# State space groups: one weighted decay matrix per head in place of two, and x left unweighted

## What is computed

```python
xdt = x * dt[..., None]
decay = segsum_exp(a_dt)
cb = jnp.einsum('bclgn,bcsgn->bcgls', c, b)
y_diag = jnp.einsum('bcgls,bcgrls,bcsgrp->bclgrp', cb, decay, xdt)
decay_states = jnp.exp(a_cs[..., -1:] - a_cs)
states = jnp.einsum('bclgn,bcgrl,bclgrp->bcgrpn', b, decay_states, xdt)
...
y_fwd = ssd_scan(xs, dt[:, :, 0], a[0], bs, cs)
y_bwd = fl(ssd_scan(fl(xs), fl(dt[:, :, 1]), a[1], fl(bs), fl(cs)))
y = y_fwd + y_bwd + xs * d_skip.astype(jnp.float32).reshape(G, R, 1)
```

## Time and profile before

| | |
|---|---|
| median of 3 runs | 1942.93 us (1938.41 to 1943.11) |
| profiled execution, its own time | 1937.86 us |
| its span (first to last instruction) | 1936.1 us |
| granted TensorE clock, mean | 0.982 |
| PE busy | 1826.7 us (94%) |
| PEld busy | 1510.2 us (78%) |
| DVE busy | 901.8 us (47%) |
| ACT busy | 856.2 us (44%) |
| POOL busy | 854.7 us (44%) |

### The profile page before, as it was taken

One profiled execution on the slowest core, in us unless ns is written; L12 is line 12 of the kernel. 1 busy time (PEld: TensorE's weight loads), 2 busy tenths in 40 slices (PEclk: granted clock), 3 DMA queues, 4 the chain that ended last, 5 costly groups with the idle time before them and its releaser, 6 DMA issues.

```text
span 1936.1 us, 27496 instructions
## 1 busy us (share of the span) xinstructions
PE 1826.7 (94%) x9012; PEld 1510.2 (78%) x9012; DVE 901.8 (47%) x1308; ACT 856.2 (44%) x1796; POOL 854.7 (44%) x598
## 2 busy tenths in 40 slices
PE   5899999999899999999999999989989999999988
PEld 4688788878687878778888888867878888877766
DVE  4588887878514565223432033060171111545654
ACT  4455555555234656323443244243523332556542
POOL 4355555555553131444444444454484444441312
PEclk9999999999999999999999999999999999999989
DMA  4731211212133131333223333324232223221111
GB/s 157 122 96 56 64 59 60 61 59 59 39 108 116 34 103 38 106 107 98 76 92 95 97 97 98 101 76 150 76 94 81 87 87 100 75 90 45 54 33 55
DMA packets 46218, 159.78 MB, mean 83 GB/s; under 512 B 4763, under 2 KB 7195, under 8 KB 45884
## 3 DMA queue, kind: packets, MB, share of 16 engines
q1 hardware_dynamic: 38592, 140.53, 23.6%
q10 hardware_dynamic: 7548, 18.20, 3.8%
HBM read 152.42 MB, written 6.29 MB: 82 GB/s over the span
## 4 chain that ended last, share of the span: by engine, by line
PE 59%; issue 19%; DVE 9%; POOL 6%; ACT 2%; DVEq 0%; DMA 0%; POOLq 0%; ACTq 0%
PE main L294 48%; POOL w_lo L257 5%; DVE u_acc L1830 2%; PE aux L779 2%; PE main L322 2%; PE main L1664 1%; PE aux L611 1%; PE aux L1741 1%; PE aux L766 1%; PE aux L364 1%; PE aux L635 1%; DVE vv L2056 1%; DVE x_res L555 1%; PE aux L753 1%; POOL spare_lo L269 1%
## 5 line engine op out<-in xcount | busy, mean ns | idle before, releaser
L257 POOL TENSOR_TENSOR w_lo<-raw,w_hi 128x512 fp32r<-128x512 f32 x504 | 714.0, 1423 | 968.0 <-ACT w_hi L253 954.3
L253 ACT ACTIVATE w_hi<-raw 128x512 fp32r<-128x512 f32 x486 | 303.8, 630 | 707.8 <-PE main L294 693.9
L294 PE MATMUL main<-w_hi,a_hi 128*128 128x512 f32 x752 | 316.1, 420 | 2.3 <-ACT vv L1434 1.4
L294 PE MATMUL main<-w_hi,a_lo 128*128 128x512 f32 x752 | 298.1, 396 | 0.0
L294 PE MATMUL main<-w_lo,a_hi 128*128 128x512 f32 x752 | 297.5, 396 | 0.0
L294 PE MATMUL main<-a_hi,w_hi 128*128 128x512 f32 x576 | 231.2, 401 | 3.2 <-ACT u_raw L1193 3.2
L294 PE MATMUL main<-a_hi,w_lo 128*128 128x512 f32 x576 | 226.4, 393 | 0.0
L294 PE MATMUL main<-a_lo,w_hi 128*128 128x512 f32 x576 | 225.9, 392 | 0.0
L294 PEld LDWEIGHTS main<-w_hi,a_lo 128*128 128x128 f32 x752 | 143.5, 191 | 31.7
L294 PEld LDWEIGHTS main<-w_hi,a_hi 128*128 128x128 f32 x752 | 144.2, 192 | 29.9 <-issue 2.1
L294 PEld LDWEIGHTS main<-w_lo,a_hi 128*128 128x128 f32 x752 | 144.3, 192 | 23.7
(11 more groups left out here) (293 smaller groups left out, 3123.4 us busy)
## 6 DMA issues: line engine op xcount, KB each, us to landing
raw<-w_stream_in SPq DMA_DIRECT2D x264, 512.0 KB, 3.5
x_res<-x_in ACTq DMA_DIRECT2D x8, 512.0 KB, 5.0
rel_rows<-rel_row ACTq DMA_DIRECT2D x1, 4096.0 KB, 45.6
bias<-rel_rows ACTq DMA_DIRECT2D x2, 1536.0 KB, 8.4
out<-x_res SPq DMA_DIRECT2D x4, 512.0 KB, 2.6
bgate<-b_gate_in ACTq DMA_DIRECT2D x4, 256.0 KB, 5.2
ln_g<-ln_g_in ACTq DMA_DIRECT2D x1, 1024.0 KB, 5.4
ln_b<-ln_b_in ACTq DMA_DIRECT2D x1, 1024.0 KB, 7.5
```

Of the source, the lines that this page charges most:

```text
L253: eng.activation(w_hi[:, k, :], raw[:, k, :], ACT.Copy).then_inc(hi_done, 1)
L257: eng.tensor_tensor(w_lo[:, k, :], raw[:, k, :], w_hi[:, k, :].bitcast(F32), ALU.subtract).then_inc(lo_done, 1)
L294: mm = eng.matmul(mb[m][:, :], lhs, rhs, start=(first and k == 0 and n == 0), stop=(last and k == KT - 1 and n == 2))
```

## The change

The two directions' dt go into the matrix instead of into x: M = (dt_f * cb_m[0] + dt_b * cb_m[1]) * decay, one matrix per head, and PE multiplies it with `x_tok` itself.

- ACT: a new `scale_cb` per head, four Copy activations of 128 x 128 from SBUF to SBUF with dt of the forward direction as scale. Those of heads 0 and 1 stand on either side of `decay_exp` 3, those of heads 2 and 3 behind `w_hi` of slots 1 and 2.
- DVE: `xdt` is gone. `weigh` is four scalar_tensor_tensor of 128 x 128, a wait for the last of them, and one tensor_tensor of 128 x 512.
- PE: `pe_y` has one matmul per chunk instead of two.
- POOL: `xw` is made from `x_tok`, with `e_st` multiplied by dt once, early, by one DVE operation of 128 x 256. It waits for `x_tok` instead of `xdt`.

```diff
         def pe_y(eng, g, r, half):
             if r == 0:
                 eng.wait_ge(arg_done, g * 4 + 4)
+                eng.wait_ge(aux_free[0], g * 5 + 2)
+                eng.wait_ge(aux_free[1], g * 5 + 2)
             eng.wait_ge(t_done, g * 4 + r + 1)
             for c in range(NT):
-                for dr in range(2):
-                    x = eng.matmul(ab[c // 2][:, (c % 2) * GW + r * HP:(c % 2) * GW + r * HP + HP],
-                                   dmat[r][:, dr, c * P:c * P + P], xdt[:, dr, c, r * HP:r * HP + HP],
-                                   start=(dr == 0), stop=(dr == 1))
+                x = eng.matmul(ab[c // 2][:, (c % 2) * GW + r * HP:(c % 2) * GW + r * HP + HP],
+                               dmat[r][:, 0, c * P:c * P + P], x_tok[:, c, r * HP:r * HP + HP], start=True, stop=True)
...
+                pool.wait_ge(aux_free[0], g * 5 + 2)
+                pool.wait_ge(aux_free[1], g * 5 + 2)
+                pool.wait_ge(dt_dve, 7)
                 for dr in range(2):
-                    pool.wait_ge(xdt_done, g * 2 + dr + 1)
-                    pool.tensor_tensor(xw[:, dr].rearrange("p c (r q) -> p c r q", r=R), xdt[:, dr].rearrange("p c (r q) -> p c r q", r=R),
+                    pool.tensor_tensor(xw[:, dr].rearrange("p c (r q) -> p c r q", r=R), x_tok[:, :, :].rearrange("p c (r q) -> p c r q", r=R),
                                        per_head(e_st, 0, NT, dr, g), ALU.mult).then_inc(xw_done, 1)
...
+            def scale_cb(g, r):
+
+                if r == 0:
+                    act.wait_ge(aux_free[1], g * 5 + 1)
+                for c in range(NT):
+                    cs = slice(c * P, c * P + P)
+                    x = act.activation(dmat[r][:, 0, cs], cb_m[:, 0, cs], ACT.Copy, scale=dt_sb[:, c, bass.ds(g * R + r, 1)])
+                x.then_inc(cb_scaled, 1)
+
...
                 slots(0, 1)
+                scale_cb(g, 0)
                 decay_exp(g, 3)
+                scale_cb(g, 1)
                 if not last:
                     pick_rows(g + 1, 1 - half)
-                slots(1, 4 - half)
+                slots(1, 2)
+                scale_cb(g, 2)
+                slots(2, 3)
+                scale_cb(g, 3)
+                slots(3, 4 - half)
...
                 def weigh(r):
+                    dve.wait_ge(cb_scaled, g * 4 + r + 1)
+                    for c in range(NT):
+                        cs = slice(c * P, c * P + P)
+                        x = dve.scalar_tensor_tensor(dmat[r][:, 0, cs], cb_m[:, 1, cs], dt_sb[:, c, bass.ds(g * R + (NH + r), 1)],
+                                                     dmat[r][:, 0, cs], ALU.mult, ALU.add)
+                    ch(x)
                     dve.wait_ge(decay_done, g * 4 + r + 1)
-                    dve.tensor_tensor(dmat[r][:, :, :], cb_m[:, :, :], dmat[r][:, 1:2, :].broadcast_to((P, 2, TOK)), ALU.mult).then_inc(t_done, 1)
+                    dve.tensor_tensor(dmat[r][:, 0, :], dmat[r][:, 0, :], dmat[r][:, 1, :], ALU.mult).then_inc(t_done, 1)
...
-                dve.wait_ge(aux_free[0], g * 5 + 2)
-                dve.wait_ge(aux_free[1], g * 5 + 2)
-                for dr in range(2):
-                    dve.tensor_tensor(xdt[:, dr].rearrange("p c (r q) -> p c r q", r=R), x_tok[:, :, :].rearrange("p c (r q) -> p c r q", r=R),
-                                      per_head(dt_sb, 0, NT, dr, g), ALU.mult).then_inc(xdt_done, 1)
                 arg_min(g, 3)
```

More of the change, by code:

```diff
@@ L154, in two_blocks @@
         dmat = [at(f"dmat{h}", B0 + (20 + 4 * h) * KB, [P, 2, TOK]) for h in range(R)]
-        xdt = at("xdt", B0 + 36 * KB, [P, 2, NT, GW])
         xw = at("xw", B0 + 44 * KB, [P, 2, NT, GW])
@@ L571, in two_blocks @@
         aux_free = [sem("aux2_free"), sem("aux3_free")]
-        xdt_done, xw_done, skip_done = sem("xdt_done"), sem("xw_done"), sem("skip_done")
-        arg_done, decay_done, t_done = sem("arg_done"), sem("decay_done"), sem("t_done")
+        xw_done, skip_done = sem("xw_done"), sem("skip_done")
+        arg_done, decay_done, cb_scaled, t_done = sem("arg_done"), sem("decay_done"), sem("cb_scaled"), sem("t_done")
         centred, arg_full, arg_in, pick_set = sem("centred"), sem("arg_full"), sem("arg_in"), sem("pick_set")
@@ L1813, in _ @@
             dve.tensor_copy(rel_row[:, :], ab[3][0:NQ, :]).then_inc(rel_dve, 1)
+            dve.wait_ge(dt_act, 10)
+            dve.tensor_tensor(e_st[:, :, :], e_st[:, :, :], dt_sb[:, :, :], ALU.mult).then_inc(dt_dve, 1)
             def conv(g, taken, pair):
@@ L1947, in ssd_group @@
                     arg_min(g + 1, 2)
-            per = len(TILES) * 3 + 1 + 2 + 3 + 6 + 1
+            per = len(TILES) * 3 + 1 + 2 + 3 + 6 + 1 + R - 1 + 1
             with dve.Fori(0, 3) as gp:
```

## The result

| | before | changed |
|---|---|---|
| median | 1940.78 us (1938.41 to 1943.11, 4 runs) | 1964.7 us (1964.39 to 1965.96, 4 runs) |
| ratio | | **1.0125**, 95% interval 1.0107 to 1.0142 |
| span of the profiled execution | 1936.1 us | 1963.1 us |
| granted TensorE clock, mean | 0.982 | 0.969 |

The changed kernel is slower by 24 us in the medians and by 27 us in the two profiled spans. The sign, the range and the place were forecast: PE's wait for `f_lo` behind the last group ends at 522.58 us where it ended at 495.52, so all 27 us lie ahead of it. The forecast of 1981 us lies 16 us too high. PE has 6 us less busy time (1820.9 against 1826.7, modelled), and ACT, DVE and POOL stay under half of the span.

What follows compares the result with a forecast made beforehand. PE and DVE were taken as nearly level, with DVE's chain bounding each group from step 3 to `pe_off` 1. Late `off_t` 32, clock 7 and last group 4 gave +43 us on 1937.86: 1981 us, range 1948 to 2002.

Steps and rivals of the forecast that it cites:

- the place: Whole kernel: the time changes between 95 and 500 us; a change outside would show the prediction wrong.
- PE: worth nothing unless DVE comes earlier.: PE ahead of its wait for `off_t`: halving `pe_y` saves 27 us of work but no time by itself.
- Late `weigh` 0, +2.7.: DVE, group 2: `weigh` 0 waits for ACT's copies and starts 2.7 us later, up to +4.1.
- `weigh` +3.0, turns -0.2.: DVE, per group: four heads' `weigh` take 7.8 us against 4.8; turns lost to POOL 4.4 against 4.6.
- Convolution -0.7: DVE, first eight convolution operations: 7.4 us instead of 8.09, with two turns lost to `w_lo` instead of three.
- `off_t` +4.5 a group: End of DVE's stretch: `off_t` comes 4.5 us later in each of 7 groups, +32 us.
- The clock, +7: PE behind its longer wait for `off_t`: slow-clock loss between 0 and 13 us, taken as half, +7 us.
- Last group, +4.: Last group, where DVE's chain sets y: late `weigh` 3 and states 2 meet POOL's L1105; +4 us, ends 0 and 9.
- PE alone sets the time: Rival: DVE's 18 us are slack and PE's saving counts; -27 us, 1911 us; chance 0.02.
- faster: Rival: on DVE, `arg_min` 3 to convolution, ending the `xw` turns outweighs the rest; -17 us, 1921 us; chance 0.07.
- Mostly absorbed: Rival: DVE's delay is about 2 us a group, still slower, 1949 to 1964 us, middle 1952; chance 0.2.

Runs made afterwards that it cites:

- the half `pe_y`: Kernel before with `pe_y` for the forward direction alone, the backward share of y left out; 1956.94 us, ratio 1.0085.
- the early `xw`: Kernel before with `xw` made early from `x_tok`, `xdt` and the two-matrix `weigh` kept; 1953.63 us, ratio 1.0061.
- the gap behind step 7: Changed kernel with `pe_off` 0 moved from behind step 6 to behind step 7, nothing else; 1983.44 us, ratio 1.0231.
- the best kernel: Kernel before with the last `pe_off` behind step 8 and, in half 1, `take_arg` 2 ahead of `take_x`; 1931.72 us, ratio 0.9955.

## Why the prediction was right, and where it was off

- **"PE: worth nothing unless DVE comes earlier."** Right in direction: the time follows DVE. But it is not free either way: by the runs the saving is worth 12 us in the changed kernel and costs 16 us in the one before. This step took a longer wait to cost nothing (the clock has its own term) and left out what an early PE does to the place of the `w_lo`.
- **Late `weigh` 0, +2.7.** From `w_hi` of slot 0 to `weigh` 0 it is 1.94 us (217.56 - 215.62) where the sum had 1.78. The copies take 1.26 us a head, not the 1.14 taken from L1210. The prediction's estimate from the prices in the Trainium skill, page "ScalarE: Activation LUTs", section "What ACT_TABLE_LOAD costs", was 0.29 us each and 1.26 a head; the trace agrees to the hundredth, and the nearest row of before was the worse guide.
- **`weigh` +3.0, turns -0.2.** Together 14.3 us from `weigh` 0 to the convolution; measured 14.03 in group 2 (14.60 in group 3). A head alone takes 1.78 us (229.81 to 231.59) where the sum had 1.95. The small operations start 0.26 us apart as L1852 did, and the turns lost come to 0.6 + 2.1 + 1.0 in three heads and 0.7 in L1906: 4.4 us, as forecast.
- **Convolution -0.7: a term too few.** The first half is 7.42 us against 7.4. The second half, which the sum left alone without a reason, fell from 6.40 to 5.38, and by 1.0 to 1.2 us in every group: 7 us in all, for the reason shown above, that POOL has nothing to do while PE stands.
- **`off_t` +4.5 a group.** Seen from the group's first `pe_y` it is +4.8 in group 2 and +4.0 in group 3 (26.16 us against 22.2), which looks like a hit. But `pe_y` is not on the chain. On the chain, from `x_tok`, `off_t` comes later by 3.4 us in group 2 and 3.8 in group 3, and the last piece of `pe_off` is later by 4.8, 8.4, 11.9, 15.6, 19.0, 22.8 and 25.8 us from group 0 to 6: 3.7 a group, where the sum had 4.5 and another 1 for the clock. The 0.8 under the sum's 4.5 is the second half of the convolution, less a little by which the other terms came out higher.
- **The clock, +7: the step that failed.** The prediction put most of the long wait at `off_t` and a loss in half of the groups behind it. The wait came one step earlier, at `pe_off` 0; its slow stretch lies under DVE's convolution and costs nothing: `off_t` to the next `x_tok` is 17.1 and 20.1 us in turn in both kernels. The step behind the last `pe_arg`, slow in two groups of three before, no longer runs slow; it lies behind the work that `x_tok` waits for and gave the chain nothing either.
- **Last group, +4.** 27.0 less 25.8 is +1.2. The sum is then 25.8 + 1.2 against 32 + 7 + 4: of the 16 us, 7 are the clock's loss that did not come, 7 the second half of the convolution, less 1 for what the other terms came out higher, and 3 the last group. The sum was 43 where 27 came; the range of 1948 to 2002 was wide enough to hold both.
- **The rivals.** "PE alone sets the time" and "faster" are denied by the result itself, and in the kernel before by the half `pe_y` and by the early `xw`. "Mostly absorbed" reached 1964 and so ends beside the measured time, but for reasons of its own that did not hold: small operations every 0.15 us, two turns lost. They start every 0.26 us and four are lost.

Open: it was not shown what makes the clock fall behind one wait and not behind another. The gap of 2.1 to 2.2 us at the last `pe_arg` is followed by a slow stretch at 200.57 and 306.14 before (0.60 and 0.63) and by none at 411.66 in the same run (1.00), and by none at 209.13, 321.88 and 434.51 in the changed kernel (1.00 each). That all three were fast there was in no forecast. Of the 18.7 us that the gap behind step 7 cost, 3.9 lie in the last group and were not followed. The new wait for `xw` in the best kernel was not pursued.

## What to carry to other kernels

Take work off the engine that the chain of waits runs through, not the one with the highest share; work taken off its partner becomes a gap, and a gap can cost more than the work did. Before trading one wide operation for several narrow ones on an engine that takes turns with another at SBUF, count the instructions of the other that fall into the stretch. When a gap can't be removed, put it ahead of work that is hidden. Divide the period at two events on the chain and sum each part in every trace: the total alone does not tell lost turns from a slow clock.

## What was not expected of the hardware

- Less work on TensorE made a kernel slower by 16 us. After gaps of 3.5 to 5.1 us in that run the next stretch had a granted clock of 0.50, with matmuls 0.43 us apart instead of 0.23; a piece of `pe_off` took 2.08 us instead of 1.13. The length of the gap alone does not tell: with the early `xw`, gaps of 3.00 us at 240.75 and 350.01 were followed by a clock of 1.00 and one of 2.48 us at 183.83 by 0.57. The Trainium skill, page "TensorE: Matmul & The Clock Gate", section "HAM oscillation — how this bites in real kernels", tells of a kernel whose bursts of matmuls each start at the lower clock after a wait; the runs here agree, though it was a saving on TensorE, and no transfer, that made the wait.
- A slow stretch is free or costly by its place: moving the gap by one step of 12 matmuls, where it also got longer, changed the time by 18.7 us.
- TensorE's wait relieved VectorE: with no `w_lo` to write, GpSimd took no turns, and the second half of the convolution took 5.38 us instead of 6.40, in all seven groups.
- Of the turns lost between VectorE and GpSimd, a part came back at another place in each order of the work that was tried. A small operation of 0.34 us took up to 1.43 us beside a `w_lo`, four times its length.
